# Attention outputs of two query blocks in one pass of the value weights, and the branch and mix stages in one block

## Chip, cores, metric

One core of a Trainium2 chip runs the whole layer. The metric is the device time of one execution in microseconds; lower is better. TensorE is called PE, its weight loads PEld, VectorE DVE, ScalarE ACT, GpSimd POOL, and SyncE, which issues the DMAs, SP.

## What is computed

One decoder layer over 16 meta tokens and 1024 tokens, width 1024. Cut to what matters:

```python
proj = rms_norm(h) @ w_in             # q, k, v of two attentions, an indexer, two gates
# 8 heads (dim 64), stick-breaking, in query blocks of 128:
a = where(visible, exp(log_sigmoid(z) + excl), 0);  o_sb = a @ v
# 8 heads (dim 64), sparse: 256 keys of each query selected by the indexer's score
p = softmax(where(selected, q k^T / 8, -inf));      o_ds = p @ v
merged = gate_sb * (o_sb @ w_branch_sb) + gate_ds * (o_ds @ w_branch_dsa)
h = h + rms_norm(merged @ w_out)
h = h + rms_norm(relu(rms_norm(h) @ w1)**2 @ w2)
```

All is float32. The kernel multiplies in a reduced-precision float32 format (fp32r): every operand is split into a rounded part (`hi`) and a remainder (`lo`), and a product is hi·hi + hi·lo + lo·hi.

## The kernel before, in words

The kernel has stages, each in a block of instructions for all engines; the end of a block is a barrier over the engines.

**Norm and projection.** x is normed, turned and split into x_hi, x_lo. A planner cuts the projection into chunks (`project`, L604); the first eleven units of 128 columns run by themselves, beside the indexer's score (L615). The others are filler for the attention's steps.

**Attention: 128 jobs in steps.** A job is one head and one block of 128 queries; 64 jobs are of the stick-breaking kind (SB), then 64 of the sparse kind (DS). Within a head the blocks come in the order 7, 0, 6, 1, 5, 2, 4, 3; block i sees 16 + 128(i+1) keys. The loop over steps j is written out for every engine in the same order:

- PE: `scores(j)` (L649, L650; two PSUM banks, up to three chunks), filler projections (first part, SB steps only), `turn(j-2)`: 128x128 transposes of the weights (L665), every eighth step the values of the next head (L632), filler (second part), `product(j-3)` (L691). In `product` the stationary operand is one value tile, 128 keys x 64, and the moving one the turned weights of 128 queries; three matmuls a tile (v_hi·pt_hi, v_hi·pt_lo, v_lo·pt_hi). The last tile of every block holds 16 keys.
- ACT: in SB steps two sigmoids of the scores; `round_weights(j-2)` (L801) makes pt_hi from the transposes' bank; in DS steps `exponent(j)` (L791); `output(j-3)` copies the 64x128 result, in SB to o_st (L818), from where SP spills it to DRAM, in DS to o_pair (L825).
- DVE: in SB steps `stick` (L1018 and L1021); in DS steps `logits(j)` (L1037), which adds the mask `sel` (bf16) and takes the row minimum; `rest_weights(j-2)` (L1065) makes pt_lo. In the first 62 steps DVE also runs the threshold search for the 256 keys (`select`, above all L960), dealt out evenly over the steps by the planner's costs.
- POOL takes remainders of weight units and of the SB outputs that SP reloads from DRAM (RELOAD steps).

`work(j)` is the planner's cost of a step on PE and sets how much filler each step gets; `dve_work(j)` does the same for the search.

**Branch.** Eight units k: 48 matmuls of 512 columns each (L279), DVE multiplies by two gates (L1191, L1192), POOL adds the halves (L1169), ACT rounds to m_hi (L1181), DVE takes m_lo (L1194). The block ends with a barrier.

**Mix, norm, MLP.** Block of its own. PE multiplies m by w_out, tiles 0 and 1 of the tokens together while the rows k of w_out arrive (L1291); ACT rounds each row (L1380), POOL takes its remainder (L1279). Then norms, turns (L1308) and the MLP (L1315, L1291).

```python
for j in range(NJ + 3):                      # PE
    if j < NJ: scores(j)
    for n, kt in FILL[j][0]: project(n, kt)
    if 2 <= j < NJ + 2: turn(j - 2)
    ...
    for n, kt in FILL[j][1]: project(n, kt)
    if j >= 3: product(j - 3)
```

## Time and profile before

| What | us |
|---|---|
| median of 3 runs (1830.69 to 1832.0) | 1830.84 |
| profiled execution, its own time | 1829.87 |
| span of the instructions in it | 1828.0 |
| attention steps | 190 to 925 |
| of these SB steps with filler | 190 to 735 |
| of these DS steps | 735 to 925 |
| branch | 926 to 1013 |
| mix, norms, MLP | 1022 to 1828 |

The page says of PE's granted clock `PEclk9999999999999999999999899999999999999999` in 40 slices. "Busy" counts each matmul from start to end; since matmuls overlap in the array, the distance between two starts, not the duration, is what one costs the stream.

### The profile page before, as it was taken

Reading aid. Unit: us, or ns where it says so; the run is one execution under the profiler, and the core shown is the slowest. Engines: PE = TensorE matmul, PEld = TensorE weight load, DVE = VectorE, ACT = ScalarE, POOL = GpSimd, SP = SyncE. Lnnn points to the kernel's source line nnn. Section 1 sums busy time; section 2 is a strip of 40 time slices with the busy share of each in tenths; the row PEclk is TensorE's granted clock in tenths of the full one; section 3 lists DMA queues with packets and bytes.
Section 4 is the critical chain, followed back from the end, with each engine's and each line's share of the span. In section 5 each row is a group of like instructions: output and inputs, shape, how many; then the busy total and the mean of one; then the engine's idle time right before and its main releaser. Section 6 shows DMA issues by size and latency. Waiting matters only on the chain. (4 is left out here: it accounts for less than half of the span.)

```text
span 1828.0 us, 25501 instructions
## 1 busy us (share of the span) xinstructions
PE 1760.5 (96%) x10088; PEld 1499.4 (82%) x10088; DVE 1019.5 (56%) x1698; ACT 664.1 (36%) x1316; POOL 398.5 (22%) x174
## 2 busy tenths in 40 slices
PE   5999999999999999899999899999999999999998
PEld 4899888899878878788888688888888888888886
DVE  5287788999999997577744244322222222222225
ACT  5366444444444444577731333212111120203032
POOL 1111312321111111111024600403122231304033
PEclk9999999999999999999999899999999999999999
DMA  4564424523423423444134431202021111202023
GB/s 167 162 189 140 131 75 125 149 84 109 111 68 97 115 67 104 110 99 95 42 139 150 150 115 70 92 12 81 23 70 37 56 47 46 60 33 81 12 80 138
DMA packets 65582, 170.53 MB, mean 93 GB/s; under 512 B 9320, under 2 KB 23976, under 8 KB 65464
## 3 DMA queue, kind: packets, MB, share of 16 engines
q1 hardware_dynamic: 65464, 168.91, 30.6%
q8 instruction: 80, 1.31, 0.3%
q14 instruction: 38, 0.31, 0.1%
HBM read 126.47 MB, written 42.41 MB: 92 GB/s over the span
## 5 line engine op out<-in xcount | busy, mean ns | idle before, releaser
L604 PE MATMUL bk<-x_hi,w_hi 128*128 128x512 f32 (+2 forms) x832 | 309.1, 372 | 1.2 <-PEq L288 1.2
L604 PE MATMUL bk<-x_lo,w_hi 128*128 128x512 f32 (+2 forms) x832 | 298.5, 359 | 0.0
L604 PE MATMUL bk<-x_hi,w_lo 128*128 128x512 f32 (+2 forms) x832 | 297.9, 358 | 0.0
L269 POOL TENSOR_TENSOR w_lo<-w_raw,w_hi 128x1024 fp32r<-128x1024 f32 x53 | 131.5, 2481 | 477.7 <-ACT w_hi L265 477.6
L1404 ACT ACTIVATE relu<-bank 128x1024 f32<-128x1024 f32 x32 | 32.9, 1029 | 504.8 <-PE bank L1315 504.8
L1315 PE MATMUL bank<-m_hi,w_hi 128*128 128x512 f32 x512 | 199.5, 390 | 0.0
L1315 PE MATMUL bank<-m_hi,w_lo 128*128 128x512 f32 x512 | 199.2, 389 | 0.0
L1315 PE MATMUL bank<-m_lo,w_hi 128*128 128x512 f32 x512 | 199.2, 389 | 0.0
L960 DVE TENSOR_SCALAR_CACHE_REDUCE sel<-sc,st_bits 128x272 bf16<-128x272 f32 (+6 forms) x217 | 184.2, 890 | 0.9
L1485 DVE TENSOR_TENSOR acc<-acc,bank 128x1024 f32<-128x1024 f32 x56 | 68.4, 1221 | 192.5 <-PE bank L1291 191.7
L604 PEld LDWEIGHTS bk<-x_hi,w_hi 128*128 128x128 f32 x832 | 158.9, 191 | 17.0 <-issue 1.3
L604 PEld LDWEIGHTS bk<-x_hi,w_lo 128*128 128x128 f32 x832 | 158.0, 190 | 17.4
L1279 POOL TENSOR_TENSOR w_lo<-w_raw,w_hi 128x1024 fp32r<-128x1024 f32 x32 | 82.9, 2597 | 405.0 <-ACT w_hi L1380 405.0
L604 PEld LDWEIGHTS bk<-x_lo,w_hi 128*128 128x128 f32 x832 | 158.4, 190 | 13.3
L1472 DVE TENSOR_TENSOR sq<-relu 128x1024 f32<-128x1024 f32 x32 | 39.2, 1225 | 227.9 <-ACT relu L1404 227.9
L1065 DVE TENSOR_TENSOR pt_lo<-bk,pt_hi 128x512 fp32r<-128x512 f32 (+2 forms) x224 | 120.2, 572 | 69.3 <-ACT pt_hi L801 67.8
L691 PE MATMUL bk<-pt_hi,v_hi 128*64 128x128 f32 (+1 forms) x704 | 149.5, 239 | 1.7 <-ACT o_st L818 1.6
L801 ACT CAST pt_hi<-bk 128x512 fp32r<-128x512 f32 (+2 forms) x224 | 101.6, 499 | 135.5 <-PE bk L665 134.7
L691 PE MATMUL bk<-pt_lo,v_hi 128*64 128x128 f32 (+1 forms) x704 | 137.8, 223 | 0.0
L691 PE MATMUL bk<-pt_hi,v_lo 128*64 128x128 f32 (+1 forms) x704 | 137.5, 222 | 0.0
L1315 PEld LDWEIGHTS bank<-m_hi,w_lo 128*128 128x128 f32 x512 | 96.1, 188 | 20.0
L1315 PEld LDWEIGHTS bank<-m_hi,w_hi 128*128 128x128 f32 x512 | 96.1, 188 | 19.8
(182 smaller groups left out, 3537.8 us busy)
## 6 DMA issues: line engine op xcount, KB each, us to landing
w_raw<-w_units SPq DMA_DIRECT2D x99, 512.0 KB, 3.7
raw<-w_units SPq DMA_DIRECT2D x24, 512.0 KB, 3.5
k_hi<-k_d SPq DMA_DIRECT2D x32, 260.0 KB, 5.0
k_lo<-k_d SPq DMA_DIRECT2D x32, 260.0 KB, 5.9
q_st<-q_d SPq DMA_DIRECT2D x32, 256.0 KB, 4.3
g_d<-stage_hi SPq DMA_DIRECT2D x32, 256.0 KB
gate<-g_d SPq DMA_DIRECT2D x16, 512.0 KB, 4.5
v_raw<-v_d SPq DMA_DIRECT2D x16, 260.0 KB, 7.3
```

Source lines behind the costliest of these rows:

```text
L269: pool.tensor_tensor(w_lo[:, s], w_raw[:, s], w_hi[:, s].bitcast(F32), ALU.subtract).then_inc(lo_done, 1)
L604: mm = pe.matmul(pj[b][:, 0:c1 - c0], w[:, s, kt, :], a[:, kt, c0:c1], start=kt == 0 and k == 0, stop=kt == KT - 1 and k == 2)
L691: mm = pe.matmul(bk[o_bank(j)][0:DH, 0:P], v[0:r, g % 2, c, :], w[0:r, j % 2, c, :], start=m == 0 and k == 0, stop=m == len(tiles) - 1 and ...
L801: act.copy(pt_hi[:, j % 2, 4 * k:4 * k + m, :], bk[TP_BANK[n]][:, 0:m * P].rearrange("p (c k) -> p c k", c=m)).then_inc(tp_hi, 1)
L960: op(dve.tensor_scalar(sel[:, BOFF[b]:BOFF[b] + KEYS[b]], sc[:, blk(b)], cand[:, j:j + 1], None, ALU.is_ge, ALU.add, accum_out=cnt[:, j:j ...
L1065: dve.tensor_tensor(pt_lo[dst], bk[TP_BANK[n]][:, 0:m * P].rearrange("p (c k) -> p c k", c=m), pt_hi[dst].bitcast(F32), ALU.subtract).then ...
L1279: pool.tensor_tensor(unit_lo(v), raw_ring[(v - V0) % 3], unit_hi(v).bitcast(F32), ALU.subtract).then_inc(lo_done, 1)
L1315: mm = pe.matmul(m1_ps[n][:, c * HALF:(c + 1) * HALF], w[s][:, kt, :], a[:, kt, c * HALF:(c + 1) * HALF], start=kt == 0 and i == 0, stop=k ...
L1404: act.activation(relu8[:], m1_ps[n][:], ACT.Relu).then_inc(relu_done, 1)
L1472: dve.tensor_tensor(sq[:], relu8[:], relu8[:], ALU.mult).then_inc(sq_done, 1)
L1485: dve.tensor_tensor(acc[:, t], acc[:, t], m2_ps[g][:], ALU.add).then_inc(acc_done, 1)
```

## The change

Products are formed for pairs of query blocks, (6,7), (0,1), (4,5), (2,3). The stationary operand `v_hl` is 128 keys x 128 columns: 64 of values' rounded part and 64 of remainders. The moving operand is 256 queries of pt_hi, then of pt_lo: two matmuls a tile of keys ("slot"), which also adds the lo·lo term. The keys are cut anew: slot 0 holds the 16 meta tokens, the others 128 tokens each; a slot that only the later block sees moves 128 queries. The result is 128x256, and its two halves of 64 rows are summed: in SB after the reload from DRAM, by POOL; in DS by DVE (`add_bottom`), after ACT has copied the upper half. `PRODUCTS` deals the pieces of four pairs over steps h+5 to h+11 of a head whose jobs start at step h; the loops run two steps longer. The mask moves into `sc` (float32) and the search writes its comparison to `counted` (uint8). Values come in two DMAs, on 128 partitions. The planner's `work` has new costs. The branch block and the mix block are one block: what waited at the barrier waits on semaphores, and the last POOL add is done by DVE.

```diff
 def groups(i):
-    tiles = [(c, min(P, KEYS[i] - c * P)) for c in range(-(-KEYS[i] // P))]
+    tiles = [(0, META, 0)] + [(c + 1, P, META + c * P) for c in range(i + 1)]
+def pieces(g):
+    h, cuts = 8 * g, []
+    for n, (start, halves) in enumerate(((5, 2), (7, 1), (9, 2), (11, 1))):
+        e, o = PAIRS[n]
+        slots = list(range(o + 2))
+        if halves == 2:
+            m = (len(slots) + 1) // 2
+            cuts += [(h + start, 1, 4 * g + n, slots[:m]), (h + start + 1, 0, 4 * g + n, slots[m:])]
+        else:
+            cuts += [(h + start, 0, 4 * g + n, slots)]
+    return cuts
 def work(j):
-    keys = [KEYS[JOBS[x_][2]] if 0 <= x_ < NJ else 0 for x_ in (j, j - 2, j - 3)]
-    return 0.89 * keys[0] + 0.9 * keys[1] + 1.41 * keys[2] + 850
+    keys = [KEYS[JOBS[x_][2]] if 0 <= x_ < NJ else 0 for x_ in (j, j - 2)]
+    return 0.89 * keys[0] + 0.9 * keys[1] + 245 * sum(len(x_[1]) for part_ in PRODUCTS[j] for x_ in part_) + 600
...
-                def product(j):
...
-                        for k, (v, w) in enumerate(((v_hi, pt_hi), (v_hi, pt_lo), (v_lo, pt_hi))):
-                            mm = pe.matmul(bk[o_bank(j)][0:DH, 0:P], v[0:r, g % 2, c, :], w[0:r, j % 2, c, :], start=m == 0 and k == 0,
-                                           stop=m == len(tiles) - 1 and k == 2)
+                def product(k, slots):
...
+                        if slot <= e + 1:
+                            dst, cols = o_part(k), slice(2 * P * slot, 2 * P * slot + 2 * P)
+                        else:
+                            dst, cols = o_part(k)[:, P:2 * P], slice(pt_at(o, slot), pt_at(o, slot) + P)
+                        for w in (hi, lo):
+                            mm = pe.matmul(dst, v_hl[0:r, g % 2, slot, :], w[0:r, cols], start=slot == 0 and w is hi,
+                                           stop=slot == o + 1 and w is lo)
...
-                for j in range(NJ + 3):
+                for j in range(NJ + 5):
                     if j < NJ:
                         scores(j)
+                    for k, slots in PRODUCTS[j][0]:
+                        product(k, slots)
...
-                    if j >= 3:
-                        product(j - 3)
+                    for k, slots in PRODUCTS[j][1]:
+                        product(k, slots)
...
+                        act.copy(o_pair[(g - H) // 2][r:r + DH, pair_cols(k)], o_part(k)[0:DH]).then_inc(top_done, 1)
...
+                def add_bottom(k):
+                    g, r = k // 4, DH * (k // 4 % 2)
+                    dst = o_pair[(g - H) // 2][r:r + DH, pair_cols(k)]
+                    dve.wait_ge(top_done, k + 1 - 4 * H)
+                    dve.tensor_tensor(dst, dst, o_part(k)[DH:P], ALU.add).then_inc(o_free, 1)
...
-                            op(dve.tensor_scalar(sel[:, BOFF[b]:BOFF[b] + KEYS[b]], sc[:, blk(b)], cand[:, j:j + 1], None, ALU.is_ge, ALU.add,
+                            op(dve.tensor_scalar(counted[:, blk(b)], sc[:, blk(b)], cand[:, j:j + 1], None, ALU.is_ge, ALU.add,
...
+                            pool.wait_ge(or_in, 64 * (p + 1))
+                            pool.tensor_tensor(o_raw[0][:], o_raw[0][:], o_raw[1][:], ALU.add).then_inc(or_sum, 1)
...
             @block.tensor
             def _(pe):
+                for k in range(KT):
+                    u = U_BRANCH + k
+                    pe.wait_ge(lo_done, u + 1)
+                    if k >= 2:
+                        pe.wait_ge(br_free, k - 1)
...
                         if t == 0:
                             pe.wait_ge(lo_done, U_OUT + k + 1)
+                            pe.wait_ge(ml_done, k + 1)
...
+                pe.wait_ge(br_free, KT - 1)
                 for k in range(KT):
                     mix_tile(0, (k,))
                     mix_tile(1, (k,))
+                pe.wait_ge(br_free, KT)
...
+                    round_unit(act, u + 2, u % 2, (u + 2) // 2)
+                    if k == KT - 1:
+                        round_ring(V0)
+                        round_ring(V0 + 1)
+                    act.wait_ge(add_done, k + 1)
...
+                    if k == KT - 1:
+                        dve.wait_ge(br_free, KT)
+                        dve.tensor_tensor(gated[:, k % 2, 0], gated[:, k % 2, 0], gated[:, k % 2, 1], ALU.add).then_inc(add_done, 1)
```

## Rows read from the trace of the kernel before

**Rows 1.** The page, part 1: busy time, share of the span, instructions
```profile
PE 1760.5 (96%) x10088; PEld 1499.4 (82%) x10088; DVE 1019.5 (56%) x1698; ACT 664.1 (36%) x1316; POOL 398.5 (22%) x174
```

**Rows 2.** Windows: length, busy of each engine, granted clock, DMA share, GB/s
```profile
190.00:712.00 522.00, 509.97 (x3362) 441.25 (x3363) 480.50 (x874) 227.94 (x520) 107.42 (x56) 0.99 0.36 105
735.00:765.00 30.00, 24.11 (x209) 20.72 (x208) 15.31 (x40) 15.61 (x38) 2.37 (x1) 0.89 0.38 94
765.00:925.00 160.00, 157.01 (x1596) 140.45 (x1596) 116.31 (x329) 119.62 (x302) 16.72 (x7) 1.00 0.36 81
855.00:876.30 21.30, 20.90 (x215) 18.74 (x214) 15.94 (x45) 15.33 (x42) 1.87 (x1) 1.00 0.39 88
```

**Rows 3.** Waits of DVE, 230 to 730: us in total, times, longest
```profile
DVE pt_lo L1065 <- ACT pt_hi L801: 34.8, 32, 6.5
```

**Rows 4.** Waits of DVE, 745 to 925
```profile
DVE n_buf L1037 <- PE bk L650: 22.0, 25, 1.9
DVE pt_lo L1065 <- ACT pt_hi L801: 19.8, 26, 2.0
```

**Rows 5.** Timeline of PE, one product and the scores behind it: start, us, instruction
```profile
842.96 0.22 PE L691 MATMUL bk<-pt_lo,v_hi 128*64 128x128 f32 x1
...
844.27 0.22 PE L691 MATMUL bk<-pt_hi,v_lo 128*64 128x128 f32 x1
844.43 0.27 PE L691 MATMUL bk<-pt_hi,v_hi 16*64 16x128 f32 x1
844.54 0.22 PE L691 MATMUL bk<-pt_lo,v_hi 16*64 16x128 f32 x1
844.60 0.22 PE L691 MATMUL bk<-pt_hi,v_lo 16*64 16x128 f32 x1
844.75 0.44 PE L649 MATMUL bk<-k_hi,q_st 128*128 128x392 f32 x1
845.03 0.34 PE L650 MATMUL bk<-k_lo,q_st 128*128 128x392 f32 x1
```

**Rows 6.** Timeline of PE, scores of 144 and of 264 keys on 128-column weights
```profile
814.79 0.28 PE L650 MATMUL bk<-k_lo,q_st 128*128 128x144 f32 x1
814.90 0.29 PE L665 MATMUL bk<-idf,a_buf 128*128 128x128 f32 x1
...
917.24 0.28 PE L649 MATMUL bk<-k_hi,q_st 128*128 128x264 f32 x1
917.36 0.29 PE L650 MATMUL bk<-k_lo,q_st 128*128 128x264 f32 x1
```

**Rows 7.** Groups by line and form, 765 to 925: busy us, mean ns, idle before
```profile
L825 ACT COPY o_pair<-bk 64x128 f32<-64x128 f32 x60 | 15.3, 256 | 8.7 <-PE bk L691 7.8
L1065 DVE TENSOR_TENSOR pt_lo<-bk,pt_hi 128x256 fp32r<-128x256 f32 x15 | 6.3, 419 | 1.8 <-ACT pt_hi L801 1.1
```

**Rows 8.** Groups by line on DVE, 230 to 730
```profile
L960 DVE TENSOR_SCALAR_CACHE_REDUCE sel<-sc,st_bits 128x656 bf16<-128x656 f32 (+6 forms) x207 | 176.6, 894 | 0.8
L994 DVE TENSOR_SCALAR sel_tmp<-sel_tmp,st_bits 128x272 f32<-128x272 f32 (+6 forms) x7 | 3.9, 557 | 0.1
L1003 DVE TENSOR_SCALAR sel<-sel_tmp 128x272 bf16<-128x272 f32 (+6 forms) x7 | 3.5, 499 | 0.2
```

**Rows 9.** Timeline from the last branch matmuls to the first of the mix
```profile
1012.77 0.61 PE L279 MATMUL br<-o_hi,w_lo 128*128 128x512 f32 x2
1013.42 1.04 ACT L265 CAST w_hi<-w_raw 128x1024 fp32r<-128x1024 f32 x1 [4.91 <-PE br L279]
1021.97 1.19 PE L1291 MATMUL bank<-w_hi,m_hi 128*128 128x512 f32 x2 [8.59 <-PEq L1133]
1025.41 4.72 POOL L1279 TENSOR_TENSOR row_lo<-w_raw,row_hi 128x1024 fp32r<-128x1024 f32 x2
```

**Rows 10.** The chain that ended last: start, us, what
```profile
1021.97 35.70 PE bank L1291 x144
...
1058.54 10.90 PE bank L1291 x48
```

More of the change, by code:

```diff
@@ L107 @@
 RELOAD = [NJ // 2 + 6 + 10 * p_ for p_ in range(4)]
-PAIR_AT = [NJ // 2 + 16 * (p_ + 1) + 3 for p_ in range(3)] + [NJ + 1]
+PAIR_AT = [NJ // 2 + 16 * (p_ + 1) + 4 for p_ in range(3)] + [NJ + 1]
+PRODUCTS = [[[], []] for _ in range(NJ + 5)]
+PRODUCT_END = {}
+for g_ in range(2 * H):
+    for step_, part_, k_, slots_ in pieces(g_):
+        PRODUCTS[step_][part_].append((k_, slots_))
+        PRODUCT_END[k_] = step_
+OUT_AT = [[k_ for k_, step_ in PRODUCT_END.items() if step_ == j_] for j_ in range(NJ + 6)]
 TPN, TP_BANK = {}, []
@@ L164 @@
 FILL, due_, spent_ = [], 0.0, 0.0
-for j_ in range(NJ + 3):
+for j_ in range(NJ + 5):
     parts_ = []
@@ L544, in _ @@
                             store(n)
-                    if j >= 3 and j - 3 < NJ and JOBS[j - 3][0] == SB:
-                        spill(j - 3)
+                    for k in OUT_AT[j]:
+                        if k < 4 * H:
+                            spill(k)
                     if j % NB == 1 and j // NB + 1 < 2 * H:
@@ L847, in _ @@
                 round_values(0)
-                for j in range(NJ + 3):
+                for j in range(NJ + 5):
                     if j < NJ and JOBS[j][0] == SB:
@@ L1091, in _ @@
                 search, spent, due = select(), 0.0, 0.0
-                for j in range(NJ + 4):
+                for j in range(NJ + 6):
                     if 1 <= j < NJ + 1 and JOBS[j - 1][0] == SB:
@@ L1106, in _ @@
                         rest_weights(j - 2)
+                    for k in (OUT_AT[j - 1] if j else ()):
+                        if k >= 4 * H:
+                            add_bottom(k)
                     if j % NB == 4 and j // NB + 1 < 2 * H:
@@ L1276, in _ @@
             def _(pool):
+                for k in range(KT):
+                    if k < KT - 1:
+                        pool.wait_ge(br_free, k + 1)
+                        pool.tensor_tensor(gated[:, k % 2, 0], gated[:, k % 2, 0], gated[:, k % 2, 1], ALU.add).then_inc(add_done, 1)
+                    rest_unit(pool, U_BRANCH + k + 2, (U_BRANCH + k) % 2)
                 for v in range(V0, N_UNITS):
```

325 lines of the change are left out of this document (162 added, 163 removed).

## The prediction

> **What bounds the kernel now.** I read the busy times first: PE is busy 96% of the span and the next engine, DVE, 56% [rows 1]. Such a mean hides the stages, so I split it by windows [rows 2]. While the search runs (190 to 712) PE is busy 510 of 522 us, but DVE is busy 480.5: it has only 41.5 us to spare. In the DS steps (765 to 925) PE is busy 157 of 160 us, DVE 116 and ACT 120. One head's eight steps take 21.3 us there, with DVE at 15.94 and ACT at 15.33. The waits say who holds whom: DVE stood 34.8 us in the SB steps for pt_hi [rows 3], which comes from PE's transposes through ACT, and in the DS steps 22.0 us for scores and 19.8 us for pt_hi [rows 4]. So PE sets the pace in both stages and the others follow, DVE closely. From 1021.97 on the chain that ended last is PE with hardly a gap [rows 10]; ahead of it lies a hole of nine microseconds [rows 9].
>
> **The price of a product now.** The reader should look at starts. From 842.96 to 844.27 are 22 matmuls in 1.31 us, 0.06 us each [rows 5]. Then comes the 16-key tile: 0.16 to its first start, 0.11, 0.06, and 0.15 to the scores, whose own first step of 0.28 is 0.10 over what 392 columns would take between 0.12 for 264 and 0.227 for 512 [rows 6, 10]. Against a steady 0.06 the detour through 16 rows costs 0.10 + 0.05 + 0.09 + 0.10, about 0.33 us a job. A head has 8 jobs with 2 to 9 tiles: 44 tiles, 36 of them full, 132 matmuls. That is 132 x 0.06 + 8 x 0.33 = 10.6 us.
>
> **The price after.** Pairs have 9, 3, 7 and 5 slots: 24 slots, 48 matmuls a head. Of them 32 are full with 256 columns, 8 are the meta slot with 256 columns, and 8 move 128 columns. The nearest rows on 128-column weights: 264 columns took 0.12 us from start to start, and 144 took 0.11 [rows 6]. The weights changed at each of them, so the load is in the price. I take 0.12 for 256 columns and 0.11 for 128: 40 x 0.12 + 8 x 0.11 = 5.7 us. The 16-row detour stays, once per pair: 4 x 0.33 = 1.3. Sum 7.0 us a head, 3.6 us less. Lower bound of the matmul price: 0.11, upper: 0.13; that is +-0.5 us a head.
>
> 144 columns cost nearly what 264 do [rows 6], so something other than the moving columns holds the short one. The Trainium skill, "TensorE: Matmul & The Clock Gate", section "LDWEIGHTS (loading the stationary operand)", puts a load at its columns divided by 1.2 GHz, an estimate of 107 ns for 128 columns and 53 ns for the old 64. By that rule the new product has no reserve: load and stream are equally long, and its figure adds to the doubt of rival 3 and changes no term here.
>
> **SB steps (190 to 735).** 60 of the 64 products lie here, 7.5 heads: 27 us less on PE. DVE doesn't shrink. Its 480.5 us in 522 leave 41.5, of which 34.8 were the wait for pt_hi; a rest of some 7 is issue time. If PE needs 27 less, the search stage has 495 us, and DVE fills 488 of it: 98.5%. Its work is dealt out evenly, but stick and search pieces differ in length from step to step, and each time that DVE is late PE waits for a_done or tp_free. I put that friction at 7 us: **-20 us**. The ends: all 27 (nothing lost) and 8. The low end is where the comparisons get dearer: written as uint8 they are not in the trace. The nearest rows are the same widths written as f32, 557 ns, and as bf16, 499 ns [rows 8]; 58 ns more on 207 comparisons would be 12 us, and a gain of as much can't be excluded. I take zero: the comparisons take 894 ns where the f32 writers of the same widths take 557, so what is written doesn't set their pace.
>
> **DS steps (735 to 925).** 8.5 heads of products lie here, up to 30 us. What comes beside PE: ACT makes 4 copies of 256 columns a head in place of 8 of 128 at 256 ns [rows 7], which is no more than before. DVE gets 4 `add_bottom` a head. The nearest row is the 256-column subtraction from PSUM, 419 ns [rows 7]: 1.7 us, so DVE goes from 15.9 to 17.6 us a head, where PE needs 21.3 - 3.6 = 17.7. Ends for one add: 0.28 and 0.69 us, the one below 128 columns' worth and 512 columns' worth; 1.1 to 2.8 us a head. The float32 mask in `logits` I cost at nothing, since scores come from PSUM in f32 already; by the 58 ns above 14 logits instructions a head would be 0.8 us at most. Two engines at 17.6 and 17.7 that hand work to each other each step can't both be full. DVE now idles 5.4 us a head; I let it keep 1.5, which gives 19.1 and a rounded gain of 2.2. Steps 0 and 4 of a head carry no product now, so behind the transposes PE meets the scores' two banks at once. Over 7.5 heads: -16.5. The first head (735 to 765) takes 30 us in place of 21, part of it at half clock (0.89 over the stretch) and behind spills on SP; with fewer spills ahead of the head's loads I give it -3.5. Together **-20 us**; ends -5 (DVE keeps most of its idle time) and -30.
>
> The product comes one to two steps later after its transposes than before, so it waits less for pt_lo; the price is two more steps at the end. There the last piece is pair (2,3), 10 matmuls with a detour, 1.5 us against 1.2, then a longer copy and an add of 0.42 ahead of the barrier: **+1 us**, ends 0 and 2. SP issues more: values in two DMAs, reloads in four, spills half as many; I cost it at nothing, since DMA is busy for 36% of the DS steps [rows 2]; without that cover the values of a head would be late, as a wait of PE. POOL adds 4 sums of 2.4 us, with nothing behind them that PE needs before the branch.
>
> **The mix.** The last branch matmul's turn ends at 1013.22 (1012.77 and two of 0.227), the mix starts at 1021.97 [rows 9]: 8.75 us. Its first 144 matmuls take 35.70 us and 48 later ones 10.90, 0.227 each [rows 10], so 35.70 - 32.7 = 3.0 us more are lost to the clock after the hole. Gone are 11.75 us at most. What is late next: weight unit 1 of w_out can be rounded only behind the last branch matmul: 0.2 + 1.04 on ACT and 2.36 on POOL (half of 4.72) make 3.6 us, and PE wants it after 12 matmuls, 2.7 us. So PE waits 0.9. Behind it POOL delivers a row each 2.36 us where PE uses one in 2.72, so it holds. m_lo of the last unit needs five operations of 1024 columns in a row on DVE and ACT; even at POOL's 2.36 each that is 12 us, and PE arrives after 19. The x and gain loads go out later, but have 20 us until tile 0 ends. **-10.8 us**, ends -7 (loads of the ring late once or twice) and -11.75.
>
> **Sum.** -20 - 20 + 1 - 10.8 = -49.8 against the profiled execution's own 1829.87 (span 1828.0 and 1.9 around it): 1780. The median shown lies 1.0 above that execution, so 1781. Ends added up: -68.75 and -18.
>
> **Rivals.**
> 1. *DVE becomes the bound* (0.20). The comparisons or the add cost their upper ends: SB -8, DS -6, mix and tail -10: 1807. For it: 98.5% and 17.6 of 17.7. Against: its waits of 34.8 and 41.8 us are slack that goes first.
> 2. *All of PE's time comes back* (0.10): -27 - 30 - 11: 1763. The DS steps' low slack speaks against it.
> 3. *Slower: the weight load shows.* Place: every product matmul. From 264 to 512 columns 248 more cost 0.107 us, so 256 columns stream for 0.11; a load of 128 columns is at most the 0.11 that 144 columns cost. In a row they make 0.22: 40 x 0.22 + 8 x 0.17 + 1.3 = 11.5 us a head, 0.9 more than now, 14 in all, with 4 of new stalls 18, less 10 of mix and tail: 1838. It decides from 0.21 us a matmul on, where (10.6 - 1.3)/48 = 0.19 and the mix's gain over 768 matmuls are used up. The 264-column scores with fresh weights at 0.12 speak against it [rows 6]. 0.03.
> 4. *Slower: PE's clock falls in the DS steps.* In 735 to 765 PE was busy 24 of 30 us and the granted clock was 0.89, with stretches at half; at 98% busy it was 1.00 [rows 2]. A head of 17.7 us of PE work at 1.2 GHz takes 35: from three heads on the gain is gone, 1832 and more. The same page of the Trainium skill, section "HAM oscillation — how this bites in real kernels", warns of idle gaps between bursts. Here single gaps should stay near a microsecond. 0.03.
> 5. *The mix gives nothing*, because PE waits on the ring where it waited at the barrier (0.04): 1791, inside the range.
>
> **How the numbers follow.** The forecast, 1766 to 1796, has 0.60. The range 1766 to 1800 leaves out the upper part of rival 1, most of rival 2 and the slower ones, some 0.2. A measurement here tells 0.2%, 3.7 us, from no change. Faster 0.94, same 0.02, slower 0.04.
>
> **What would show it.** PE's product matmuls are 768 in place of 2112, starts 0.12 apart; SB steps end near 715 with DVE over 97% busy; a DS head takes 19 us; no hole at the mix and full clock there. It is wrong if starts are 0.15 or more apart, if DVE's waits stay while PE gets waits for DVE, or if the granted clock falls in the DS steps.

## Result, and the profile after

The changed kernel takes 1812.15 us (median of 4 runs, 1810.42 to 1815.18) against 1831.28 for the kernel before in the same comparison: ratio 0.9896, 95% interval 0.9881 to 0.9912. It is faster, by 19.1 us, where I had said 50 and a range of 1766 to 1800. The profiled execution took 1812.03 us, span 1810.2. Its page, part 1, and the clock line of part 2, as [rows 1]:

```profile
PE 1716.2 (95%) x8744; PEld 1448.9 (80%) x8744; DVE 1030.0 (57%) x1730; ACT 649.8 (36%) x1252; POOL 408.6 (23%) x177
PEclk9999899999999999999999999999999999999999
```

PE's busy time fell by 44 us and the span by 18, so 26 us less work came out as idle time of PE. Where, the starts of the scores in the trace's timeline tell. This table is my reading of them, in us of the profiled executions (e3 to e16 are experiments below). The first four columns run between first scores; "end" runs from step 127's scores to the first branch matmul, "branch" from there to the first mix matmul, "rest" from there to the last matmul. The last column says for how many us of the six DS heads PE's granted clock was half (1.2 GHz in place of 2.4).

| kernel | SB steps | first DS head | six DS heads | 7 last steps | end | branch | rest | half clock in the six |
|---|---|---|---|---|---|---|---|---|
| before | 546.4 | 30.4 | 131.5 | 18.0 | 9.2 | 95.9 | 797.0 | 0 |
| after | 539.3 | 21.1 | 131.3 | 20.5 | 11.6 | 87.2 | 797.5 | 3.4 |
| after - before | -7.1 | -9.3 | -0.2 | +2.5 | +2.4 | -8.7 | +0.5 | |
| e3 short search, after | 521.2 | 22.3 | 135.4 | 18.0 | 11.6 | 88.7 | 797.4 | 13.6 |
| e5 values later | 525.2 | 20.9 | 134.7 | 17.7 | 11.6 | 87.2 | 797.6 | 13.6 |
| e6 no additions | 539.1 | 21.0 | 124.0 | 16.5 | 11.2 | 87.2 | 797.8 | 3.4 |
| e9 less product, after | 538.9 | 20.3 | 132.1 | 16.9 | 12.2 | 89.6 | 797.3 | 20.4 |
| e10 less product, before | 546.3 | 29.2 | 122.7 | 16.2 | 8.6 | 95.9 | 796.4 | 0 |
| e11 POOL adds | 535.7 | 22.0 | 127.5 | 18.7 | 14.9 | 90.0 | 797.7 | 0 |
| e12 e11 and e16 | 525.2 | 21.0 | 135.1 | 17.7 | 15.7 | 89.2 | 796.5 | 20.4 |
| e13 additions twice | 535.7 | 22.1 | 146.4 | 21.2 | 15.0 | 89.5 | 797.0 | 30.6 |
| e14 same dose, before | 546.5 | 30.8 | 132.8 | 18.2 | 9.3 | 95.9 | 796.3 | 0 |
| e15 e6 and e9 together | 538.0 | 20.2 | 122.4 | 15.3 | 10.2 | 87.1 | 797.7 | 13.6 |
| e16 the best | 524.9 | 21.0 | 131.3 | 18.0 | 14.9 | 89.4 | 796.6 | 3.4 |

The steps also began 2.0 us later in this execution (192.6 for 190.6). In the experiments on the changed kernel they began at 190.7 to 192.5, so most of that is not the change's.

**The product costs what was forecast.** Timeline of PE, as [rows 5]: start, us, instruction.

```profile
858.01 0.28 PE L755 MATMUL bk<-pt_hi,v_hl 128*128 128x256 f32 x1
858.12 0.28 PE L755 MATMUL bk<-pt_lo,v_hl 128*128 128x256 f32 x1
858.25 0.28 PE L755 MATMUL bk<-pt_hi,v_hl 128*128 128x256 f32 x1
858.37 0.28 PE L755 MATMUL bk<-pt_lo,v_hl 128*128 128x256 f32 x1
```

The starts lie 0.12 us apart. DVE's two uncertain terms, the comparison that writes uint8 (groups by line, 230 to 730, as [rows 8]) and the addition (its line's own view, duration min/median/max in ns), came out as taken too:

```profile
L1023 DVE TENSOR_SCALAR_CACHE_REDUCE counted<-sc,small 128x272 uint8<-128x272 f32 (+6 forms) x210 | 178.3, 891 | 0.9
...
L1140 DVE TENSOR_TENSOR o_pair<-o_pair,bk x32: 422/424/427, 754.3 to 915.7; 64x256 f32<-64x256 f32 x32
```

So neither price was wrong: 891 ns for 894, 0.42 us for 0.42.

**SB steps.** The window that answers to [rows 2], and the waits of 230 to 730 (us in total, times, longest):

```profile
190.00:712.00 522.00, 495.99 (x2769) 426.04 (x2769) 480.75 (x886) 222.05 (x496) 109.24 (x56) 0.97 0.37 110
...
DVE pt_lo L1126 <- ACT pt_hi L868: 38.0, 26, 7.1
...
PE bk L690 <- DVE pt_lo L1126: 15.3, 8, 4.4
PE bk L708 <- ACT n_buf L850: 5.7, 7, 1.4
```

PE is down to 496 us of 522, but DVE did no more in this window than before (480.75 for 480.50), and its wait for pt_hi grew from 34.8 [rows 3] to 38.0. A third row is the odd one: PE waits for DVE at the values of the next head (L690), 15.3 us in eight waits. In the kernel before the same place had:

```profile
PE bk L632 <- DVE pt_lo L1065: 6.0, 8, 2.4
```

And the granted clock is 0.97 for 0.99. One such place in the timeline of the changed kernel:

```profile
235.26 1.16 DVE L1023 TENSOR_SCALAR_CACHE_REDUCE counted<-sc,small 128x912 uint8<-128x912 f32 x1
...
236.35 1.28 DVE L1126 TENSOR_TENSOR pt_lo<-bk,pt_hi 128x512 fp32r<-128x512 f32 x2
237.08 0.50 PEld L690 LDWEIGHTS bk<-idf,v_raw 64*128 64x128 f32 x4 [3.31 <-DVE pt_lo L1126]
...
238.15 0.49 PE L661 MATMUL bk<-x_lo,w_hi 128*128 128x348 f32 x1
238.45 0.49 PE L661 MATMUL bk<-x_hi,w_lo 128*128 128x348 f32 x1
238.73 0.49 PE L661 MATMUL bk<-x_hi,w_hi 128*128 128x344 f32 x1
```

In step h+4 PE turns block 6's weights, two groups, and then the values, two halves: four fills of a ring of three banks (4, 5, 6). The fourth needs the first back, and DVE gives it back with pt_lo of this same step, which stands behind the step's share of the search. PE waited 3.3 us, and then its filler ran with starts 0.29 us apart, where 0.16 is usual: half the clock. In all, 26 us of the SB steps ran at half clock, for 7 in the kernel before. Of the eight SB heads, the four without a half-clock stretch took 1.1 to 3.8 us less than before, the four with one from 0.7 less to 2.0 more.

**DS steps.** The same stretch of 21.3 us as the last of [rows 2], and the waits of 745 to 905, as [rows 4]:

```profile
855.00:876.30 21.30, 17.68 (x127) 14.68 (x127) 17.37 (x51) 15.65 (x38) 0.00 (x0) 1.00 0.40 88
...
DVE pt_lo L1126 <- ACT pt_hi L868: 19.9, 32, 1.4
DVE n_buf L1099 <- PE bk L709: 2.4, 4, 1.5
...
PE bk L708 <- DVE small L1099: 11.0, 8, 1.6
```

PE 17.68 and DVE 17.37 us: the forecast for a head was 17.7 and 17.6. Only the head hardly got shorter. The heads took 21.35 and 22.49 us by turns before; at full clock they now take 20.65 to 20.9 and 22.5 to 22.8. DVE's wait for scores is gone (22.0 to 2.4), its wait for pt_hi is what it was (19.8 to 19.9), and PE now waits for DVE's logits to free a score bank.

**The mix.** Timeline, as [rows 9], and the chain that ended last from 1000 on:

```profile
1003.18 0.61 PE L313 MATMUL bank<-o_hi,w_lo 128*128 128x512 f32 x2
...
1003.63 0.62 PE L1329 MATMUL bank<-w_hi,m_hi 128*128 128x512 f32 x2
...
1006.29 2.14 DVE L1501 TENSOR_TENSOR gated<-gated 128x1024 f32<-128x1024 f32 x1
1007.29 3.40 POOL L1306 TENSOR_TENSOR row_lo<-raw,row_hi 128x1024 fp32r<-128x1024 f32 x1
...
1007.40 0.74 PE L1329 MATMUL bank<-w_hi,m_hi 128*128 128x512 f32 x2 [0.89 <-POOL w_lo L303]
```

```profile
1007.35 13.77 POOL row_lo L1306 x5
1021.14 9.00 DMA w_raw<-w_units
1030.16 1.05 ACT w_hi L1421
```

The hole is gone: the next matmul follows at the pace of the stream. The wait of 0.9 for w_lo of weight unit 1 is the one that I named. The chain then goes over POOL's rows and a weight DMA to ACT, which rounds an MLP weight ahead of tile 0's norm. PE's waits in this stage:

```profile
PE bank L1347 <- DVE nn L1532: 2.2, 2, 1.4
PE bank L1329 <- POOL w_lo L303: 0.9, 1, 0.9
PE bank L1329 <- POOL row_lo L1306: 0.6, 2, 0.3
```

In the kernel before, nn cost 1.4 in one wait and the others nothing, so these rows hold 2.3 us that are new. The rest of the program took 797.5 us where 797.0 less the 3.0 of clock would be 794.0: they are 2.3 of the 3.5 missing.

### The profile page after: what moved, and what is told of

It reads as the page before. It is cut to its first block and busy times, and to the rows that moved or that the text cites. A ratio compares the mean times of both kernels' runs of the same rounds, so it can differ in the third digit from the quotient of the medians.

```text
span 1810.2 us, 22709 instructions
## 1 busy us (share of the span) xinstructions
PE 1716.2 (95%) x8744; PEld 1448.9 (80%) x8744; DVE 1030.0 (57%) x1730; ACT 649.8 (36%) x1252; POOL 408.6 (23%) x177
## 5 line engine op out<-in xcount | busy, mean ns | idle before, releaser
L1023 DVE TENSOR_SCALAR_CACHE_REDUCE counted<-sc,small 128x272 uint8<-128x272 f32 (+6 forms) x217 | 184.3, 891 | 0.9
L1552 DVE TENSOR_TENSOR acc<-acc,bank 128x1024 f32<-128x1024 f32 x56 | 68.4, 1221 | 192.5 <-PE bank L1329 191.7
L661 PEld LDWEIGHTS bk<-x_hi,w_hi 128*128 128x128 f32 x832 | 160.9, 193 | 16.2 <-issue 1.3
L661 PEld LDWEIGHTS bk<-x_lo,w_hi 128*128 128x128 f32 x832 | 160.9, 193 | 13.6
L755 PE MATMUL bk<-pt_hi,v_hl 128*128 128x256 f32 (+2 forms) x384 | 109.8, 311 | 6.6 <-ACT o_st L885 3.5
L1354 PEld LDWEIGHTS bank<-m_lo,w_hi 128*128 128x128 f32 x512 | 96.1, 188 | 19.9
L1354 PEld LDWEIGHTS bank<-m_hi,w_hi 128*128 128x128 f32 x512 | 96.1, 188 | 19.8
L724 PE MATMUL bk<-idf,a_buf 128*128 128x128 f32 (+1 forms) x704 | 99.8, 276 | 4.0 <-DVE pt_lo L1126 3.1
```

The source lines that it names most:

```text
L661: mm = pe.matmul(pj[b][:, 0:c1 - c0], w[:, s, kt, :], a[:, kt, c0:c1], start=kt == 0 and k == 0, stop=kt == KT - 1 and k == 2)
L724: mm = pe.transpose(bk[TP_BANK[n]][0:r, m * P:(m + 1) * P], a_buf[:, j % 3, col:col + r], idf[:])
L755: mm = pe.matmul(dst, v_hl[0:r, g % 2, slot, :], w[0:r, cols], start=slot == 0 and w is hi, stop=slot == o + 1 and w is lo)
L1023: op(dve.tensor_scalar(counted[:, blk(b)], sc[:, blk(b)], cand[:, j:j + 1], None, ALU.is_ge, ALU.add, accum_out=cnt[:, j:j + 1]))
L1354: mm = pe.matmul(m1_ps[n][:, c * HALF:(c + 1) * HALF], w[s][:, kt, :], a[:, kt, c * HALF:(c + 1) * HALF], start=kt == 0 and i == 0, stop=k ...
L1552: dve.tensor_tensor(acc[:, t], acc[:, t], m2_ps[g][:], ALU.add).then_inc(acc_done, 1)
```

## The experiments

**The two halves of the change.** e1 is the kernel before with the branch and the mix in one block, e2 the changed kernel with the two blocks of before.

```diff
-            pool.tensor_tensor(gated[:, k % 2, 0], gated[:, k % 2, 0], gated[:, k % 2, 1], ALU.add).then_inc(add_done, 1)
...
+                pe.wait_ge(br_free, KT - 1)
                 for k in range(KT):
                     mix_tile(0, (k,))
                     mix_tile(1, (k,))
```

> The kernel before with the branch and mix blocks made one, products as before. Theory: the merge is worth what the two traces show between the first branch matmul and the end of PE (892.9 us before, 884.7 after), 8.2 us, and it stands by itself: 1823. Rival: part of it comes from or is lost to the new place of the buffers and the shorter attention ahead, then it gives under 5 or over 11 us.

> The changed kernel with the branch and mix in two blocks as before, so the pairs alone. Theory: the parts add up, so this is worth what is left of the 19, some 10 to 11 us: 1820 to 1821. The hole of 8.7 us at the mix and the half clock behind it are back. Rival: the parts interact and this gives under 6 or over 15 us.

Measured: e1 1822.2, ratio 0.9951 (0.9936 to 0.9965), as expected; e2 1817.04, ratio 0.9926 (0.991 to 0.9943), 3 us below what I expected. The mix brings 9.7 us by the medians and the pairs 14.9; the two add up to 5.5 more than the whole's 19.1, about the width of one of these intervals (5 to 6 us). The mix did nearly what I said. The pairs, forecast at 39, are where the error is.

**Is it the search on DVE?** The last 11 of its 31 bits are left out, so the selection is coarser and DVE has less to do; once in the changed kernel, once in the kernel before.

```diff
-                    for bit in reversed(range(BITS)):
+                    for bit in range(BITS - 1, 10, -1):
-SEARCH_NS = 278e3
+SEARCH_NS = 202e3
```

> The changed kernel, leaving out the last 11 of the 31 bits of the threshold search (77 of its 217 counting instructions, the selection is coarser) and with the planner's cost for the search lowered in proportion. VectorE has some 80 us less in the stick-breaking steps, TensorE the same. Theory A: in the changed kernel VectorE, full with the search, sets the length of these steps; then they fall from 539 us towards TensorE's own 481 plus its small losses, to 500 to 510, and the whole to 1775 to 1785; the waits for pt_lo at the values step vanish. Rival B: the three banks of the transposes make TensorE wait at the values whatever the search costs; then these steps stay over 530 and the whole over 1803.

> The kernel before with the same part of the search left out. Theory A: here TensorE has 27 us more of its own in these steps (508), so they fall less, from 546 to 526 to 534 us, and the whole to 1811 to 1820; the difference to the changed kernel with the same search then shows the products' full 27 us in these steps. Rival B: it falls as much or as little as the changed kernel does.

Measured: e3 1796.97, ratio 0.9812 (0.9792 to 0.9831), SB steps 521.2 for 539.3; e4 1828.07, ratio 0.998 (0.997 to 0.9991), SB steps 543.7 for 546.4. The same relief is worth 18.1 us to the changed kernel and 2.7 to the one before. Both fell by less than theory A said (to 500 to 510, and to 526 to 534). PE's wait at the values fell from 15.3 to 4.5 us. In e3 these steps had no more half clock than in the kernel before (6.8 us), and PE was busy for 507.05 us of them, for 534.37 before: the 27 us less that I had forecast. So DVE held the changed SB steps; this doesn't say yet whether by its amount of work or at one place.

**By amount or at one place?** The values of the next head are turned at step h+5, where the weights (block 1) need one group and not two. DVE's work stays as it is.

```diff
-                    if j % NB == 4 and j // NB + 1 < 2 * H:
+                    if j % NB == 5 and j // NB + 1 < 2 * H:
                         values(j // NB + 1)
```

> The changed kernel with the values of the next head turned one step later, where TensorE transposes one group of the weights and not two. The stick-breaking steps took 539 us in the changed kernel, with 15.3 us of waits of the values for pt_lo and 26 us at half clock. Theory A (a late VectorE is felt there because two groups and two halves of values want four of three banks in one step): the waits of the values for pt_lo fall under 5 us, the half clock goes with them, these steps take 522 to 530 us, the whole 1798 to 1805. Rival B (VectorE is simply full): the wait moves to another instruction, the steps stay within 4 us of 539.

Measured: 1801.9 (1797.22 to 1802.52), ratio 0.9841 (0.9824 to 0.9857). Its window and its waits from 230 to 715:

```profile
190.00:712.00 522.00, 504.38 (x2848) 432.94 (x2849) 495.30 (x894) 227.75 (x510) 117.08 (x57) 0.98 0.38 111
...
PE bk L708 <- ACT n_buf L850: 11.0, 7, 3.7
...
PE bk L690 <- DVE pt_lo L1126: 1.4, 1, 1.4
...
DVE pt_lo L1126 <- ACT pt_hi L868: 15.5, 8, 4.4
```

It was the place. With the whole search still there, the SB steps fell to 525.2, DVE filled 495.3 us of 522 where it had filled 480.75, and its wait for pt_hi fell to 15.5. Of the 13.9 us that the wait at the values gave back, 5.3 went into another one at the first scores of a head (5.7 to 11.0), and 17 us of the SB steps still ran at half clock. They are 21.2 us shorter than before: what I had forecast for them. The profiled execution was the fastest of the four (1797.22), but e12 and e16, which have the same move in the SB steps, show the same length (525.2 and 524.9). The six DS heads took 134.7 for 131.3; this isn't shown to be the move's doing, since e3, whose DS steps are those of the changed kernel, took 135.4 with the same 13.6 us at half clock.

**The DS steps: the additions.** e6 leaves out DVE's 32 additions of the lower halves, so the sparse outputs lack the values' remainders; e7 does the addition ahead of the weights' remainder.

```diff
-                        act.copy(o_pair[(g - H) // 2][r:r + DH, pair_cols(k)], o_part(k)[0:DH]).then_inc(top_done, 1)
+                        act.copy(o_pair[(g - H) // 2][r:r + DH, pair_cols(k)], o_part(k)[0:DH]).then_inc(o_free, 1)
...
-                            add_bottom(k)
```

In e7 the same three lines stand higher:

```diff
                         logits(j)
+                    for k in (OUT_AT[j - 1] if j else ()):
+                        if k >= 4 * H:
+                            add_bottom(k)
...
                         rest_weights(j - 2)
-                    for k in (OUT_AT[j - 1] if j else ()):
-                        if k >= 4 * H:
-                            add_bottom(k)
```

> The changed kernel, leaving out the 32 additions of the lower halves in the sparse steps (that part of the output is missing), 0.42 us each on VectorE. Six heads in the middle of these steps took 131.3 us, as before the change. Theory A (the chain of scores, VectorE, transposes, ScalarE, VectorE is the bound and the add lies on it): they fall by the 4 x 0.42 us a head or more, to 119 to 122 us. Rival B (the pace is set by the two score banks alone): under 3 us less.

> The changed kernel with the same additions ahead of the remainders of the step's weights on VectorE, where it waits for ScalarE anyway, and not behind them. Theory A: most of the additions' cost is hidden, the six heads take 121 to 126 us. Rival B: under 3 us less than 131.3, since VectorE's order doesn't matter.

Measured: e6 1799.41, ratio 0.9826 (0.9806 to 0.9846); six heads 124.0 for 131.3. e7 1812.07, ratio 0.9895 (0.9875 to 0.9915); six heads 131.2. The additions are 6 x 4 x 0.42 = 10.2 us of DVE's time in six heads, and 7.3 of them show; theory A had the six heads at 119 to 122. Moved within the step (e7), the addition makes no difference to the time of the whole; head by head there is a small one (below).

**The score banks.** PE waits for logits to free one of two banks; here scores rotate over three, and the transposes keep three in place of four.

```diff
-    ring = (4, 5, 6) if j < NJ // 2 + 2 else (4, 5, 6, 0)
+    ring = (4, 5, 6)
...
-                        dst = bk[2 + z % 2][:, 0:c1 - c0]
+                        dst = bk[(2, 3, 0)[(z - NZ_SB) % 3]][:, 0:c1 - c0]
```

> The changed kernel with three PSUM banks for the scores in the sparse steps, the third taken from the transposes' ring of four. Theory B of the runs before (two score banks hold TensorE, whose waits for the scores' reader are 11.4 us and those of its weight loads 18.2): these waits fall under 5 us and the six heads take 120 to 125 us. Theory A (the chain through VectorE): the wait moves to the transposes' banks, and the six heads stay within 4 us of 131.

Measured: 1829.84 (1823.88 to 1849.89), ratio 1.0005 (0.9974 to 1.0036): worse than the changed kernel by 17.7 us, six heads 139.9 in its profile, a fast one (1823.9), with 17.0 us at half clock. Neither theory foresaw that. Its waits of PE, 745 to 905:

```profile
PE bk L693 <- DVE pt_lo L1131: 9.0, 6, 1.8
PE bk L729 <- DVE pt_lo L1131: 8.3, 7, 1.2
PE bk L713 <- DVE small L1104: 5.1, 7, 0.9
```

The wait for the score bank fell from 11.0 to 5.1, and the waits for pt_lo at the values and the transposes, 6.8 us in the changed kernel, are 17.3. A bank moved from one ring to the other moves the wait; it doesn't show which engine holds the pace.

**Less for PE, in both kernels.** e9 leaves out, in the DS steps of the changed kernel, the pt_lo matmul of the slots that both blocks share; e10 leaves out the v_lo matmul of full tiles in the kernel before. The remainders' terms are missing from the sparse outputs.

```diff
                         for w in (hi, lo):
+                            if w is lo and k >= 4 * H and 0 < slot <= e + 1:
+                                continue
...
                         for k, (v, w) in enumerate(((v_hi, pt_hi), (v_hi, pt_lo), (v_lo, pt_hi))):
+                            if t == DS and k == 2 and m < len(tiles) - 1:
+                                continue
```

> The changed kernel, leaving out in the sparse steps the second matmul (remainders of the weights) of every slot that both blocks see, but the meta slot: 16 matmuls of 0.12 us a head, 1.9 us of TensorE, 11.5 us in the six heads; all waits, ScalarE's and VectorE's work stay. Theory A (the chain through VectorE sets the pace): the six heads stay at 127 to 132 us. Rival C (TensorE still sets it): they take 119 to 122 us.

> The kernel before, leaving out in the sparse steps the third matmul of every full tile but the meta one and the last: 36 of 0.06 us a head, 2.1 us of TensorE, 13 us in the six heads, which took 131.5 us. It shows how much a lighter TensorE could have won without the additions and with the products after the transposes. Theory A: the chain there has less in it than after the change, so they fall by 5 to 11 us. Rival C: by all of 12 to 13 us. If they fall by under 3 us the kernel before was not bound by TensorE in these steps, and my reading of it was wrong.

Measured: e9 1806.14, ratio 0.9871 (0.9846 to 0.9895), six heads 132.1: nothing off; its two runs lie 6.9 us apart, and the profile is of the slower. e10 1817.79, ratio 0.9934 (0.9914 to 0.9954), six heads 122.7 for 131.5: 8.8 us off. In the kernel before a lighter PE pays; in the changed one nothing shows in the six heads. But e9 has a second reading: 20.4 us of its six heads ran at half clock, for 3.4 in the changed kernel and none in e10. What is left at full clock follows below.

**More for DVE, in both kernels.** The direct test: e13 makes each addition twice, e14 gives the kernel before the same dose, a 256-column subtraction in four blocks of each sparse head.

```diff
+                    dve.tensor_tensor(twin[r:r + DH, pair_cols(k)], dst, o_part(k)[DH:P], ALU.add)
                     dve.tensor_tensor(dst, dst, o_part(k)[DH:P], ALU.add).then_inc(o_free, 1)
...
+                        if t == DS and i > 3 and k == 0:
+                            two = (slice(None), j % 2, slice(0, 2), slice(None))
+                            dve.tensor_tensor(twin[:], bk[TP_BANK[n]][:, 0:2 * P].rearrange("p (c k) -> p c k", c=2), pt_hi[two].bitcast(F32), ALU.subtract)
```

> The changed kernel with each of the 32 additions in the sparse steps made twice on DVE (the first copy goes to a buffer that nothing reads): 1.7 us more of DVE work a head. The output is the same. Theory (in the sparse steps of the changed kernel the chain that comes back to DVE each step sets the time, no longer PE's stream): six heads take 131.3 + 6 x 1.7, 139 to 142 us, and the whole 10 to 14 us more than the changed kernel, near 1824. Rival (PE sets the pace in the changed kernel too, and what the leaving out of the additions gave was the pace of the output banks): within 4 us of 1812.

> The kernel before with one 256-column subtraction more on DVE in each of the blocks 7, 6, 5 and 4 of the sparse heads, written to a buffer that nothing reads: 4 x 0.42, or 1.7 us more of DVE work a head, the same dose as the changed kernel's additions. The output is the same. Theory (there PE sets the pace and DVE has 5.4 us a head to spare): the six heads stay at 131.5, up to 134, the whole within 4 us of 1831. Rival (the chain over DVE sets the pace in the kernel before as well): 10 us more, 1841 and up.

Measured: e13 1833.5 (10 runs), ratio 1.001 (0.9998 to 1.0022): 21 us above the changed kernel, six heads 146.4 for 131.3. e14 1832.8 (10 runs), ratio 1.0011 (1.0001 to 1.002): 1.8 us above, six heads 132.8 for 131.5. The same 10.2 us of DVE work cost 15.1 in one kernel, more than the theory's 8 to 11, and 1.3 in the other. (e13's profile is of its fastest run, 1828.94.) The rival of the output banks is out: no wait of PE's products for an addition stands in e13's rows or in the changed kernel's. The windows 765 to 893, some six heads, and DVE's waits in them, first of the kernel before, then of the changed one, then of e14:

```profile
765.00:893.00 128.00, 125.55 (x1267) 111.89 (x1268) 93.79 (x267) 97.55 (x245) 16.72 (x7) 1.00 0.44 101
...
DVE pt_lo L1065 <- ACT pt_hi L801: 15.1, 18, 2.0
DVE n_buf L1037 <- PE bk L650: 12.5, 16, 1.5
```

```profile
765.00:893.00 128.00, 109.49 (x759) 90.99 (x758) 102.65 (x287) 90.81 (x215) 21.36 (x9) 0.97 0.43 97
...
DVE pt_lo L1126 <- ACT pt_hi L868: 15.8, 26, 1.0
DVE n_buf L1099 <- PE bk L709: 2.1, 3, 1.5
```

```profile
765.00:893.00 128.00, 124.56 (x1254) 110.51 (x1253) 98.59 (x288) 96.62 (x240) 14.84 (x7) 1.00 0.44 101
...
DVE n_buf L1038 <- PE bk L651: 13.5, 15, 1.6
DVE pt_lo L1069 <- ACT pt_hi L802: 9.5, 9, 1.7
```

Add up DVE's row in the changed kernel: 102.65 busy and 17.9 of waits are 120.6 of 128. The addition took the place of the wait for scores. The wait for pt_hi stayed, 15.8 us in 26 short ones of 0.6: in it PE turns the weights that DVE's logits let go and ACT rounds them. The row alone doesn't prove that this time is no spare time: with the dose in the kernel before it did give way, 15.1 to 9.5 and 1.9 more at the added subtraction. The doses show it, for the changed kernel alone: there 10.2 us more cost 15.1 and 10.2 less gave 7.3, though DVE's waits add up to 17.9. That they belong to the round trip logits, scores, turn, rounding, remainder is my reading; no run changes that order.

Much of e13's 15.1 is clock: it was granted 0.92 from 755 to 885, the changed kernel 0.99. Its heads, taken singly, separate the two (below).

**Both reliefs at once.** e15 has the edits of e6 and of e9.

> The changed kernel without the 32 additions in the sparse steps and without the pt_lo matmul of the shared slots of keys there: both doses at once. The sparse outputs then lack the lower halves and the remainder terms. Leaving out the additions alone gave 1799 and six heads of 124.0 us; leaving out the matmuls alone six heads of 132.1 and 25 us at half clock. Theory (two engines that hand over to each other each step: once DVE is relieved, PE counts again): six heads of 114 to 119 us, 1790 to 1794. Rival (what PE no longer does only lowers its granted clock): six heads of 122 us or more, with over 15 us at half clock, 1797 and up.

Measured: 1794.19 (1792.91 to 1795.79), ratio 0.9801 (0.9784 to 0.9817); six heads 122.4, with 13.6 us at half clock. Neither theory's figure: with DVE relieved, the smaller product gave 1.6 us in six heads where e10's gave 8.8.

**Head by head.** The six heads can be taken apart, and those that had full clock throughout compared. Where the code of the DS steps is the same (the changed kernel, e2, e3, e16), such a head repeats within 0.04 us from run to run. The third of the six, in the changed kernel (half clock for 3.4 us of it) and in e3 (none), windows as [rows 2]:

```profile
796.41:818.38 21.97, 19.55 (x132) 16.40 (x131) 17.05 (x48) 15.21 (x37) 4.74 (x2) 0.92 0.60 134
...
778.55:799.45 20.90, 17.97 (x132) 15.04 (x131) 16.98 (x48) 15.21 (x37) 4.77 (x2) 1.00 0.63 142
```

These are the heads that ran at full clock, in us; a dash stands for one that didn't. In the row of the changed kernel the third head is e3's.

| kernel | 1 | 2 | 3 | 4 | 5 | 6 |
|---|---|---|---|---|---|---|
| before | 21.35 | 22.49 | 21.34 | 22.49 | 21.35 | 22.48 |
| e10 less product, before | 19.88 | 21.39 | 19.35 | 21.41 | 19.51 | 21.16 |
| e14 same dose, before | 21.59 | 22.83 | 21.34 | 22.83 | 21.36 | 22.82 |
| after | 20.65 | 22.77 | 20.91 | 22.52 | 20.89 | 22.53 |
| e5 values later | 20.31 | 22.84 | - | - | 20.32 | - |
| e6 no additions | 19.28 | 21.97 | 19.86 | - | 19.26 | 21.46 |
| e7 addition early | - | 22.34 | - | 22.13 | 20.51 | 22.15 |
| e9 less product | - | - | - | 22.22 | - | - |
| e11 POOL adds | 20.01 | 22.79 | 20.41 | 21.86 | 20.50 | 21.92 |
| e13 additions twice | - | - | 21.67 | - | 21.94 | - |
| e15 e6 and e9 together | 17.72 | - | 19.97 | - | 18.10 | 20.90 |

Per head, the additions left out (1.7 us of DVE) give 0.8 to 1.6, and a second set of them costs 0.8 and 1.0 in e13's two. The 1.9 us of products left out give 0.3 in the one head of e9; with the additions gone too (e15 against e6) they give 1.6, nothing, 1.2 and 0.6. In the kernel before, 2.1 us of products give 1.1 to 2.0, and 1.7 us on DVE cost 0 to 0.3. So in the changed kernel the work of either engine shows in part, where before it was almost only PE's; by an estimate from these heads two thirds of e13's 15.1 us are half clock (six times 0.9 is 5.4), and e15's 1.6 us would be some 5 at full clock. The values' move did no harm to a DS head at full clock, and the early addition gives 0.4 a head. The six heads of the changed kernel at full clock would be 130.3 us, so the clock took 1.0 of them.

**The additions elsewhere.** e11: ACT copies both halves and POOL adds them, once for two heads. e12: that, with the values at h+5 in the SB heads, and ACT rounding the second MLP unit behind tile 1's norm. e16: the last two without the first.

```diff
-                        act.copy(o_pair[(g - H) // 2][r:r + DH, pair_cols(k)], o_part(k)[0:DH]).then_inc(top_done, 1)
+                        act.copy(o_pair[(g - H) // 2][r:r + DH, pair_cols(k)], o_part(k)[0:DH])
+                        act.copy(o_bot[(g - H) // 2][r:r + DH, pair_cols(k)], o_part(k)[DH:P]).then_inc(o_free, 1)
...
+                            pool.tensor_tensor(o_pair[p][:], o_pair[p][:], o_bot[p][:], ALU.add).then_inc(top_done, 1)
...
-    if j_ % NB == 4 and j_ // NB + 1 < 2 * H:
+    if j_ % NB == (5 if j_ < NJ // 2 else 4) and j_ // NB + 1 < 2 * H:
...
-                for v in range(V0 + 2, U_MLP + 2):
+                for v in range(V0 + 2, U_MLP + 1):
                     round_ring(v)
...
+                    if t == 1:
+                        round_ring(U_MLP + 1)
```

> The changed kernel with the lower halves copied by ScalarE too (32 copies of 64x256 at 0.36 us) and added by GpSimd once per two heads, so nothing of it on VectorE but one addition behind the last barrier; the sums of two heads are scaled two steps later. Theory A: as without the additions, 131.3 us become 122 to 126 in the six heads, ScalarE's extra 1.4 us a head hidden, and the whole takes 1800 to 1804 us. Rival: ScalarE is on the same chain (it rounds what VectorE waits for), then the six heads stay over 129.

> The same as e11, with the values of the next head one step later in the stick-breaking steps alone, and with ScalarE rounding the second MLP weight unit behind the norm of token tile 1 and not ahead of that of tile 0. If the three gains add up: 1812 - 13 - 9 - 1 = 1789 us; if the sparse steps give nothing: 1798.

> The changed kernel with the next head's values turned at step h+5 in place of h+4 in the stick-breaking heads only, the sparse heads as in the changed kernel, and ACT's rounding of the second MLP weight unit behind the norm of tile 1. All is computed. Turning the values later in both halves gave 1801.9, with stick-breaking steps 14 us shorter and six sparse heads 3.4 us longer. Theory (the two moves are independent): stick-breaking steps near 525, sparse heads as in the changed kernel, 131, rest of the program about 1 us shorter: 1797, under both kernels' 1812 and 1831. Rival (what is gained in the first half comes back as half clock in the second, since the sparse heads vary by it): 1801 to 1804.

Measured: e11 1809.45, ratio 0.989 (0.9874 to 0.9907), six heads 127.5, all at full clock: 2.8 us less than the 130.3, and short of both theories. e12 1798.95 (1792.95 to 1803.71), ratio 0.983 (0.9805 to 0.9854), near the 1798 that I gave it if the sparse steps bring nothing. Its six heads took 135.1 us: the same code there as e11's, 7.6 us longer, with 20.4 us at half clock for none. e16 1798.29 (1795.14 to 1806.2), ratio 0.9827 (0.9802 to 0.9852). e11's 3.8 us in the heads are spent by its end and branch (14.9 and 90.0 for 11.6 and 87.2), which also had 13.7 us at half clock; e16, without e11's edits, shows nearly the same two (14.9 and 89.4). e16 beats both kernels: 33 us under the one before, 14 under the changed one, with SB steps of 524.9, heads of 131.3 and the wait for nn back at 1.4. Its runs overlap with those of e12 and e5, so it isn't shown to beat these.

Its runs spread over 11 us, and the profile shows a possible reason. The end of the attention, in e16:

```profile
892.27 1.78 PE L734 MATMUL bk<-idf,r_wide 128*128 128x128 f32 x8 [1.50 <-ACT r_wide L894]
...
895.09 0.41 PE L755 MATMUL bk<-pt_lo,v_hl 128*128 128x256 f32 x1
895.30 0.41 PE L755 MATMUL bk<-pt_hi,v_hl 128*128 128x256 f32 x1
```

and in the changed kernel, the same instructions:

```profile
910.68 1.09 PE L734 MATMUL bk<-idf,r_wide 128*128 128x128 f32 x8 [1.50 <-ACT r_wide L894]
...
912.35 0.28 PE L755 MATMUL bk<-pt_lo,v_hl 128*128 128x256 f32 x1
912.47 0.29 PE L755 MATMUL bk<-pt_hi,v_hl 128*128 128x256 f32 x1
```

The same two waits (0.79 and 1.50 us) stand just ahead of both. In one the clock stays full, in the other it is half for 13.7 us (starts 0.21 apart for 0.12), into the branch. That costs the end 3.3 us and the branch 2.2.

## Why the prediction was wrong

**What held.** The product price (0.12 a matmul) and with it PE's busy time (17.68 us for 17.7 in a DS head; 27 less in the SB steps where the clock is equal, e3), DVE's added work, the uint8 comparison at nothing, the hole at the mix (8.7 of 8.75) and the full clock behind it, the 0.9 of weight unit 1. Rival 3, the weight load that shows, is ruled out by the starts. The Trainium skill's figure for a load of 128 columns in "TensorE: Matmul & The Clock Gate", section "LDWEIGHTS (loading the stationary operand)", comes to an estimate of 107 ns, and the trace doesn't speak against it: 0.12 from start to start with 256 moving columns on 128 rows, and at full clock nothing near twice that but around the 16-row slot (0.20 to 0.23), whose detour had its own term.

**DS steps, 13 us short (predicted -20, measured -7.0).** The step that failed is "DVE now idles 5.4 us a head; I let it keep 1.5". It still idles 21.3 - 17.37 = 3.9 us. I had read both of DVE's waits as slack, and wrote so against rival 1. The one for scores was slack and went first. The one for pt_hi is the way over PE and ACT, and it stayed. With it the stretch of 21.3 us is 17.4 busy, 2.6 of that wait (15.8 / 6) and 1.3 of small rests. The prediction had named this as a sign of being wrong: DVE's waits stay while PE gets waits for DVE (11.0 us for logits). The clock has little part in it: at full clock the six heads would be 130.3 us, where I had 118.3 (131.5 less six times 2.2). The first head gave 9.3 where I gave it 3.5: the wait of 3.8 us for the values' DMA fell to 0.5, and two stretches at half clock, 3.4 us each, left it. The seven last steps and the end cost 4.9 where I had 1. The 2.5 of the last steps are a half-clock stretch of 6.8 us from 887.9 on: e3 and e16, with the same code there and full clock, took 18.0, as before. The 2.4 of the end stand at full clock too.

**SB steps, 13 us short (-20, measured -7.1).** The failed term is the friction, 7 us. The balance of PE and DVE over the stage was right: e5 reaches 525.2, -21.2. What was left out is the ring of three banks: one step in eight needs four fills, and then PE depends on DVE within a step. The row was there before, 6.0 us in eight waits, and I hadn't asked what it would become once PE came 27 us earlier: 15.3, plus half clock behind the long ones (19 us more of it in these steps). The term had no row behind it.

**Mix, 2.6 short.** The rows show two of POOL's remainders at 3.40 and 3.37 for the 2.36 taken, beside DVE's operations on SBUF, and tile 0's norm, late behind ACT's wait for a weight DMA: 0.6 and 0.8 us of PE's waits. The other 1.2 isn't placed.

**The clock** was rival 4, with gaps "near a microsecond". Single gaps were up to 4.4 us, and each of the four over 2 us at the values' step was followed by 3.4 or 6.8 us at half. It took its share in every stage and ruled none, so the rival's 1832 was far off. The result came nearest to rival 1, DVE as the bound (1807), but that is in part luck, since its terms were wrong: not dearer instructions, but waits that aren't slack.

## What to carry to other kernels

A waiting engine's idle time is spare only as far as the wait ends on the engine that you make faster. Where engines hand over to each other in a round within a step, part of each one's waiting is the others' share of the round; it stays when one gets faster, so two engines at 83% and 82% busy can be the bound together, and then the work of each shows in part. Also, where work passes through a ring of banks, count the fills of the fullest step: a step that needs more than the ring has ties the two engines together inside the step. And a dose of extra work, given to the same engine before and after a change, tells which kernel that engine holds. Read such doses in the stretches with equal clock: the same code took 127.5 us in six heads with none at half clock and 135.1 with 20.4.

## What the runs showed of the hardware

A wait of PE can cost more than its length. With the four waits of 2.2 to 4.4 us at the values' step of the changed kernel came stretches of 3.4 or 6.8 us at half clock; a head of 20.91 us took 21.98 with one of 3.4 us. The Trainium skill, "TensorE: Matmul & The Clock Gate", section "HAM oscillation — how this bites in real kernels", tells of the same between bursts that wait for DMAs; here the wait was for a semaphore between engines, and it was not regular: a wait of 2.4 us at the same place of the kernel before (234.3) had no such stretch, and waits of 1.5 us had one at the end of e16 and none at that of the changed kernel.

POOL's remainder of a 1024-column row took 2.39 us by itself and 3.40 where it started inside a DVE operation with two operands in SBUF (L1501, 2.14 us, where DVE's operation on a PSUM operand took 1.22). The Trainium skill, "GPSIMD Engine Reference", section "1. Specifications", says that POOL shares its SBUF interfaces with DVE, with contention when DVE reads two SBUF inputs; the trace agrees, by 1.0 us a row for POOL. In these rows it matters which of the two starts first: sixteen rows of the MLP in the kernel before, and as many in the changed one, started with 1.1 us of such an operation (`row_lo`, 2.2 us) still to go and took 3.37; the rows of the branch in which one began only after POOL's start took 2.40, though it ran for 1.2 us beside them.

What a narrower output type saves on DVE was nothing here: 891 ns for uint8, 894 for bf16, means over the same widths.
